# Alternating long and short matmuls inside an output tile of a split-precision weight stream

## What is computed

```python
for i in range(DEPTH):                      # DEPTH = 2, D_MODEL = 2048, D_FF = 5632, SEQ = 256
    h = _rmsnorm(x, norm_mix[i])
    x = x + (_mla(h, ...) if i % 2 == 0 else _stick_breaking(h, w_qkv, w_o))
    x = x + _mem_cross_attn(_rmsnorm(x, norm_mem_q[i]), _rmsnorm(mem, norm_mem_kv[i]), ...)
    x = x + _conv_ffn(_rmsnorm(x, norm_ffn[i]), ffn_w_in[i], ffn_conv_w[i], ffn_conv_b[i], ffn_w_out[i])
return _rmsnorm(x, norm_final)
```

## Time and profile before

| | |
|---|---|
| median of 3 runs | 2385.25 us (2383.45 to 2387.8) |
| the profiled execution's own time | 2386.63 us |
| its span, first to last instruction | 2384.8 us |
| TensorE busy | 2352.6 us, 99% |
| weight loads busy | 2097.3 us, 88% |
| VectorE busy | 1687.6 us, 71% |
| ScalarE busy | 1237.1 us, 52% |
| DMA | 434.55 MB, mean 182 GB/s |

### The profile page before, as it was taken

The page is one execution under the profiler, slowest core; times in us unless marked ns, Lnnn a source line. Parts: engine busy times, 40 slices in busy tenths (PEclk is TensorE's granted clock), DMA queues, the critical chain, the costliest instruction groups (busy, mean ns, idle before and its releaser), DMA issues.

```text
span 2384.8 us, 41584 instructions
## 1 busy us (share of the span) xinstructions
PE 2352.6 (99%) x14424; PEld 2097.3 (88%) x14424; DVE 1687.6 (71%) x2490; ACT 1237.1 (52%) x1872; POOL 303.5 (13%) x309
## 2 busy tenths in 40 slices
PE   9899999999999999999999999999999999999997
PEld 8799898888888888889899998889888888888886
DVE  8777678777877875555765556778778778785554
ACT  6445555655555654444555445455555556554432
POOL 6500225000000000111330000315000000001110
PEclk9999999999999999999999999999999999999999
DMA  7534554555555666555554545545555555555553
GB/s 278 188 133 141 190 176 157 191 190 185 191 188 184 193 187 211 186 190 182 184 175 163 167 166 170 191 161 172 190 185 191 188 184 192 189 183 195 191 188 124
DMA packets 122647, 434.55 MB, mean 182 GB/s; under 512 B 13488, under 2 KB 17840, under 8 KB 122544
## 3 DMA queue, kind: packets, MB, share of 16 engines
q1 hardware_dynamic: 118992, 423.94, 54.2%
q0 software_dynamic: 2016, 7.34, 1.0%
q10 hardware_dynamic: 1536, 1.85, 0.2%
HBM read 430.98 MB, written 2.10 MB: 182 GB/s over the span
## 4 chain that ended last, share of the span: by engine, by line
PE 93%; DVE 5%; ACT 1%; POOL 1%; DMA 1%; issue 0%; DVEq 0%; SPq 0%; ACTq 0%; POOLq 0%
PE bank L1391 50%; PE bank L1398 28%; PE bank L1393 3%; PE bank L1394 3%; PE bank L1413 2%; PE bank L1415 2%; PE bank L1414 2%; DVE w_lo L902 2%; DVE h L925 1%; PE bank L1482 1%; ACT w_hi L510 1%; DMA w_raw<-stream 1%; PE bank L1483 0%; PE bank L1473 0%; DVE x L968 0%
## 5 line engine op out<-in xcount | busy, mean ns | idle before, releaser
L902 DVE TENSOR_TENSOR w_lo<-w_raw,w_hi 128x1024 fp32r<-128x1024 f32 x802 | 1006.5, 1258 | 525.1 <-ACT w_hi L510 523.4
L510 ACT ACTIVATE w_hi<-w_raw 128x1024 fp32r<-128x1024 f32 x802 | 845.3, 1057 | 745.8 <-PE bank L1398 661.6
L1391 PE MATMUL bank<-h,w_hi 128*128 128x512 f32 x3360 | 1037.2, 396 | 3.2 <-DVE h L925 1.9
L1398 PEld LDWEIGHTS bank<-h,w_lo 128*128 128x128 f32 x3632 | 655.8, 188 | 137.4
L1398 PE MATMUL bank<-h,w_lo 128*128 128x256 f32 x3632 | 694.9, 279 | 0.0
L1391 PE MATMUL bank<-act,w_hi 128*128 128x512 f32 x1816 | 571.2, 396 | 0.0
L1391 PEld LDWEIGHTS bank<-h,w_hi 128*128 128x128 f32 x3360 | 521.1, 189 | 15.7 <-DVE h L925 2.1
L1398 PEld LDWEIGHTS bank<-act,w_lo 128*128 128x128 f32 x2304 | 414.3, 189 | 80.6
L1398 PE MATMUL bank<-act,w_lo 128*128 128x256 f32 x2304 | 448.5, 279 | 0.0
L1391 PEld LDWEIGHTS bank<-act,w_hi 128*128 128x128 f32 x1816 | 276.5, 189 | 0.3
L437 POOL TENSOR_TENSOR sq<-x 128x256 f32<-128x256 f32 x101 | 115.5, 1144 | 359.2 <-DVE x L968 354.2
(11 more groups left out here) (152 smaller groups left out, 1957.2 us busy)
## 6 DMA issues: line engine op xcount, KB each, us to landing
w_raw<-stream SPq DMA_DIRECT2D x802, 512.0 KB, 3.3
tmp<-mem_in POOLq DMA_DIRECT2D x14, 512.0 KB, 5.3
out<-attn SPq DMA_DIRECT2D x5, 256.0 KB, 2.7
x<-x_in SPq DMA_DIRECT2D x4, 256.0 KB, 5.3
x<-x_in SPq DMA_DIRECT2D x2, 512.0 KB, 9.2
out<-attn ACTq DMA_DIRECT2D x3, 256.0 KB, 2.2
cols<-cols_in ACTq DMA_DIRECT2D x1, 420.5 KB, 7.4
mats<-mats_in ACTq DMA_DIRECT2D x1, 320.0 KB, 7.9
```

The lines of the kernel that those rows point to most:

```text
L510: nc.scalar.activation(w_hi[:, s, :], w_raw[:, s, :], ACT.Copy).then_inc(hi_split, 1)
L902: nc.vector.tensor_tensor(w_lo[:, s, :], w_raw[:, s, :], w_hi[:, s, :], ALU.subtract).then_inc(lo_split, 1)
L1391: mm(bank[:, :], w_hi[:, s, c:c + P], a, start=first and i == 0, stop=False)
L1398: ins = mm(bank[:, 0:TOK], w_lo[:, s, c:c + P], a[:, 0:TOK], start=False, stop=last and i == len(ks) - 1)
```

## The change

In every output tile of a unit but the first (`j` above 0), where both parts of the weights are used (`parts == 2`), the matmuls are issued block by block: long, short, long, short. The first tile of each unit keeps its order. The matmuls, their operands, banks, the wait at the start of the unit and the increment at the end of each tile are the same; the sums in a bank are added in another order.

```diff
                     bank = banks[bank_of(j)]
+                    if parts == 2 and j:
+                        for i, k in enumerate(ks):
+                            c = i * width + j * P
+                            a = operand(k)
+                            mm(bank[:, :], w_hi[:, s, c:c + P], a, start=first and i == 0, stop=False)
+                            ins = mm(bank[:, 0:TOK], w_lo[:, s, c:c + P], a[:, 0:TOK], start=False, stop=last and i == len(ks) - 1)
+                        ins.then_inc(chunks_done, 1)
+                        continue
                     for i, k in enumerate(ks):
```

## The result

The changed kernel takes 2392.07 us (median of 18 runs, 2389.03 to 2394.88), the kernel before 2385.64 us (18 runs, 2382.9 to 2388.56). The ratio is 1.0023 with a 95% interval of 1.0017 to 1.0029: slower by 0.23%, 6.4 us, which is just outside what counts here as no change. The profiled execution took 2391.34 us with a span of 2389.5 us.

What follows compares the result with a forecast made beforehand. The prediction took TensorE, through its number of matmuls times their pace, to bound the kernel. Its terms summed as 0 + 0 + 0 + 0 us on the runs' median of 2385.25 us, giving 2385.3 us, range 2374 to 2394 us.

Steps and rivals of the forecast that it cites:

- the case that got most of the chance: Reordered pairs on TensorE keep 348.3 ns, 0 us, own range 7 us either way; no change within 0.2% had 0.58.
- What bounds the kernel: TensorE, busy 99% of the span at full clock; the time is the number of matmuls times their pace.
- Counts: Of 5176 long matmuls, 3754 are reordered with as many short ones: 3498 in four-tile units, 256 in stick-breaking queries and keys.
- Nothing added, no wait moved: Each tile keeps its matmuls, weight loads, bank and end increment, and each unit its one wait for `lo_split`: 0 us.
- The cover of the loads: Weight loads on TensorE: in either order two lie under long matmuls and two under short ones per tile, 0 us.
- a price of the same bank: A long matmul following a short one in the same bank was claimed to wait for no sum: 0 ns.
- The pace at a change of length: Alternating long and short matmuls on TensorE: a fixed amount on top of each, so 348.3 ns a pair stays, 0 us.
- The upper bound: Alternating pairs with long matmuls at 233 and short at 120 ns: 353 ns a pair, 18 us lost.
- the lower one: Alternating pairs with long matmuls at 226 and short at 115 ns: 341 ns a pair, 27 us saved.
- Each change of length saves: Each switch between long and short matmuls gains 3.4 ns: 344.9 ns a pair, 13 us saved, 2372 us; chance 0.17.
- The second rival: Long matmuls lose their good pace behind every short one: 353 ns a pair, 18 us lost, 2403 us; chance 0.12.
- The third, better hidden loads: Weight loads half hidden before would be hidden by alternation: part of 27 us saved, 2358 us at most; chance 0.03.

Runs made afterwards that it cites:

- runs of four and of eight: Against the kernel before, four-tile units issue four long matmuls then four short, or all eight long then eight short: 2398.17 us and 2392.83 us.
- the switch once in 16 units: Against the changed kernel, all tiles alternate except the first tile of one four-tile unit in every 16: median 2393.50 us, ratio 1.0032.
- two tiles first: Against the changed kernel, the first two of four tiles run long, long, short, short and the last two alternate: median 2400.76 us, ratio 1.0054.
- the order that always returns to the cheap pace: Against the changed kernel, four-tile units alternate throughout, but every third starts with two long, long, short, short tiles; two-tile units unchanged: median 2381.22 us, ratio 0.9979.
- The last tile alone: Against the changed kernel, three tiles run long, long, short, short and only the last of four alternates: median 2393.51 us, ratio 1.0033.

## Why the forecast was near and where it failed

The forecast was 2385.3 us with 2374 to 2394 us, and the time is 2392.07 us: inside the range, but the case that got most of the chance, no change within 0.2%, isn't the one that came. Slower by more than 0.2% had 0.16.

**What bounds the kernel: right.** TensorE is the bound before and after, and the waits keep their order. In the profiled executions with 256 columns the change in the pace of the units, times their number, gives the change in time to within about 3 us.

**Counts: right.** 3754 pairs were reordered, 3498 of them in units of four tiles.

**Nothing added, no wait moved: right.** The same number of instructions, the same waits to within 9 us of ScalarE's 670 us, which aren't on the path.

**The cover of the loads: nothing spoke against it, but it wasn't tested by itself.** Each load still starts with the matmul ahead of its own, and as many loads lie under long matmuls as before. That the number of covered loads decides nothing is supported by the two paces: the same loads under the same matmuls give 346.6 and 353.3 ns. The order of banks is the same at both paces too, and the cheap one lies below the 348.3 ns of before, so a price of the same bank shows nowhere; a small one inside both paces isn't excluded.

**The pace at a change of length: the step that failed.** The prediction read "with no trend in the length of runs. A fixed amount for each matmul is the simplest reading, and then order has no price", and took the pace of runs of two. The runs showed that the amount isn't fixed. Alternation has two paces, and their plain mean, (346.6 + 353.3) / 2 = 350.0 ns, is 1.7 ns above the 348.3 ns taken. 3498 pairs x 1.7 ns are 5.9 us, the term that should have stood in place of 0; measured are 6.4 us. The case's own range of 7 us either way held that. That the time came so near is partly luck: the pace taken lies between the two that exist, and since the first tile of each unit makes the units take turns, 5.0 ns a pair lost in one unit are followed by 1.7 ns gained in the next. The upper bound, 353 ns, was put together from separate rows and lies at the dear pace, and the lower one, 341 ns, wasn't reached.

**The rivals.** "Each change of length saves" is refuted by runs of four and of eight (350.8, 349.1 ns) and by the changed kernel itself; its 344.9 ns was never seen. The second rival had the side right, and its 353 ns is the dear pace. Its working isn't: it left the long ones at 233 ns and put the short ones at 120. In the dear cycle the long ones take 0.23, 0.24 and 0.24 us and the short ones 0.12, 0.12 and 0.11, means of 237 and 117 ns, so most of the loss is in the long ones. It had also taken this for the one pace of alternation, and it holds in half of the units. The third, better hidden loads, gave nothing.

**Why the change is slower, shown.** The first tile of a unit, which keeps its order, flips the phase; the three alternating tiles keep it. So units are cheap and dear in turn, 2.78 and 2.81 us, for a mean of 2796 ns against 2786.7 ns. Orders worked out from the flips behave as computed: the switch once in 16 units, two tiles first with all units alike, and the order that always returns to the cheap pace, the only one with all the work whose median lies below the kernel before (2381.22 us, ratio 0.9979). The last tile alone was computed wrong ahead of its run, for a transition that hadn't been seen.

**What stays open.** What in TensorE holds the phase isn't known from these runs, nor what sets it when a stage begins after a wait. The groups of runs of one and the same program show that it can differ from one execution to the next. No run took the weight loads out, so whether the time on top of the columns comes from them isn't shown either way.

## What to carry to other kernels

When one engine is busy for the whole span and an edit only reorders its instructions, count the instructions in long windows and also read the starts over several repeats: a mean of 174.2 ns a matmul can be one pace or two in turn. Run an order many times before judging it: with all tiles alternating, 12 runs gave 2380 us three times and 2392 to 2397 us nine times, and a single run would have told either story. If two paces are found, look for what flips them, since an order that always ends in the better one gets the gain in each run; here it is small, 0.2%.

## What the runs showed of the hardware

With the granted clock at full in every window, the same sequence of matmuls and weight loads ran at 346.6 or 353.3 ns a pair and stayed there for whole stages, hundreds of pairs; one tile of another order moved it from one to the other. The repeated patterns have lengths near whole multiples of 6.67 ns: 2773, 2780, 2793, 2800, 2807 and 2820 ns a unit (416, 417, 419, 420, 421 and 423 times), 1.06 us for three dear pairs, 120 ns for short matmuls alone. With 8 columns fewer in the short matmul the pace didn't fall by one fixed amount: one execution had 343.4 ns a pair in one stretch and 346.2 in another. Within a group of executions the time goes with the mean granted clock: of 23 runs of the kernel before, those at 0.997 and 0.998 took 2383.3 to 2385.8 us and those at 0.994 and 0.995 took 2386.7 to 2388.7 us. That doesn't make the groups: with all tiles alternating, two runs at the same 0.997 took 2380.4 and 2391.8 us.
